# State-space tables of both layers in one feed-forward, and a third feed-forward in seven-product form

## The reference, cut to what matters

```python
x = post_add(x, swiglu(pre(x, 0), ffn_w_in[l, 0], ffn_w_out[l, 0]), 0, 0.5)   # first feed-forward
y = token_mixer(pre(x, 1), ...)       # state-space branch + forgetting attention + gates
x = post_add(x, y, 1, 1.0)
x = post_add(x, swiglu(pre(x, 2), ffn_w_in[l, 1], ffn_w_out[l, 1]), 2, 0.5)   # second feed-forward

def swiglu(h, w_in, w_out):           # 1024 -> 2 x 2816 -> 1024
    gate, up = split(h @ w_in)
    return (silu(gate) * up) @ w_out

def s5_ssm(u, a_re, a_im, log_dt, b_re, b_im, c_re, c_im, d_skip):
    lam = complex(min(a_re, -1e-4), a_im); dt = exp(log_dt)
    lam_bar = exp(lam * dt)
    b_bar = (lam_bar - 1) / lam * b
    states = associative_scan(a2 * a1, a2 * s1 + s2)   # over 512 tokens
    return real(c @ states) + d_skip * u
```

## Time and profile before

| | us |
|---|---|
| median of 3 executions (3386.50 to 3389.12) | 3387.81 |
| profiled execution, its own time | 3392.64 |
| profiled execution, its span | 3390.8 |
| layer 1's first feed-forward: first XH matmul to the next stage's first | 1085.5 to 1468.4 |
| layer 1's second feed-forward | 1875.2 to 2241.3 |
| layer 2's first feed-forward | 2241.3 to 2623.9 |
| layer 2's second feed-forward, from its first XH matmul | about 3029 on |

### The profile page before, as it was taken

One profiled execution on the slowest core, in us unless ns is written; L12 is line 12 of the kernel. 1 busy time (PEld: TensorE's weight loads), 2 busy tenths in 40 slices (PEclk: granted clock), 3 DMA queues, 4 the chain that ended last, 5 costly groups with the idle time before them and its releaser, 6 DMA issues.

```text
span 3390.8 us, 43065 instructions
## 1 busy us (share of the span) xinstructions
PE 3330.1 (98%) x17581; PEld 2689.4 (79%) x17589; DVE 1938.0 (57%) x2745; ACT 1364.9 (40%) x2134; POOL 443.2 (13%) x343
## 2 busy tenths in 40 slices
PE   9999999999999999999999999999999999999998
PEld 6755477688888888888678899978888875879998
DVE  5555666565555635564334867665356633367775
ACT  3374456332223332224533554432323245245443
POOL 0100012222221100122012100020102210220001
PEclk9999999999999999999999999999999999999999
DMA  5412543255553334223033123333432331222232
GB/s 195 148 44 76 186 180 131 105 193 199 194 189 116 122 139 139 87 93 121 31 110 108 57 100 106 101 109 112 146 116 68 123 106 44 100 75 99 95 107 75
DMA packets 82261, 393.68 MB, mean 116 GB/s; under 512 B 8976, under 2 KB 19856, under 8 KB 51088
## 3 DMA queue, kind: packets, MB, share of 16 engines
q1 hardware_dynamic: 69936, 370.41, 30.8%
q10 hardware_dynamic: 12128, 20.52, 1.7%
HBM read 372.02 MB, written 18.87 MB: 115 GB/s over the span
## 4 chain that ended last, share of the span: by engine, by line
PE 90%; DVE 5%; ACT 2%; issue 2%; POOL 0%; DMA 0%; SPq 0%; ACTq 0%; DVEq 0%; POOLq 0%
PE pb L813 16%; PE pb L815 16%; PE pb L814 16%; PE pb L1308 4%; PE pb L1307 4%; PE pb L1306 4%; PE pb L714 2%; PE pb L781 2%; PE pb L716 2%; PE pb L1347 2%; PE pb L1348 2%; PE pb L782 2%; PE pb L1349 2%; PE pb L789 2%; PE pb L1015 1%
## 5 line engine op out<-in xcount | busy, mean ns | idle before, releaser
L2406 DVE TENSOR_TENSOR wl<-w,wh 128x2048 fp32r<-128x2048 f32 (+2 forms) x207 | 449.0, 2169 | 591.3 <-ACT wh L1568 590.7
L813 PE MATMUL pb<-XH,wh 128*128 128x512 f32 (+1 forms) x1848 | 735.4, 398 | 2.3 <-DVE wl L2406 1.6
L815 PE MATMUL pb<-XH,wl 128*128 128x512 f32 (+1 forms) x1848 | 721.3, 390 | 0.0
L814 PE MATMUL pb<-XL,wh 128*128 128x512 f32 (+1 forms) x1848 | 720.7, 390 | 0.0
L1568 ACT ACTIVATE wh<-w 128x2048 fp32r<-128x2048 f32 (+2 forms) x207 | 363.0, 1754 | 217.8 <-PE pb L815 134.5
L813 PEld LDWEIGHTS pb<-XH,wh 128*128 128x128 f32 (+1 forms) x1848 | 345.9, 187 | 83.2 <-issue 8.2
L814 PEld LDWEIGHTS pb<-XL,wh 128*128 128x128 f32 (+1 forms) x1848 | 345.9, 187 | 76.7 <-issue 4.6
L815 PEld LDWEIGHTS pb<-XH,wl 128*128 128x128 f32 (+1 forms) x1848 | 345.3, 187 | 75.6
L2393 DVE CUSTOM_DVE_ANT_0 mreg<-mreg,pr 128x1024 f32<-128x1024 f32 x144 | 196.4, 1381 | 50.4 <-DMA mreg<-in_mod_w 50.1
L813 PE MATMUL pb<-HH,wh 128*128 128x512 f32 x552 | 219.0, 397 | 0.5 <-DVE YT L3356 0.5
L814 PE MATMUL pb<-HL,wh 128*128 128x512 f32 x552 | 218.0, 395 | 0.0
(11 more groups left out here) (589 smaller groups left out, 6507.0 us busy)
## 6 DMA issues: line engine op xcount, KB each, us to landing
mreg<-in_mod_w SPq DMA_DIRECT2D x144, 512.0 KB, 4.1
w<-in_f_in SPq DMA_DIRECT2D x44, 1024.0 KB, 4.8
w<-in_f_wide SPq DMA_DIRECT2D x38, 1024.0 KB, 4.8
w<-in_w_up SPq DMA_DIRECT2D x16, 1024.0 KB, 6.0
w<-in_w_dn SPq DMA_DIRECT2D x16, 1024.0 KB, 5.9
w<-in_f_out SPq DMA_DIRECT2D x16, 1024.0 KB, 4.9
w<-in_m_g SPq DMA_DIRECT2D x16, 1024.0 KB, 4.8
w<-in_f_piece SPq DMA_DIRECT2D x32, 512.0 KB, 3.4
```

The costliest lines, as they stand in the source:

```text
L813: mm(dst, hi[:, cs], xh[:, k, :], start=k == 0, stop=False)
L814: mm(dst, hi[:, cs], xl[:, k, :], start=False, stop=False)
L815: x = mm(dst, lo[:, cs], xh[:, k, :], start=False, stop=fin)
L2406: tt(low[:, 0:s.cols], wslots[b % 3][:, 0:s.cols], h[:, 0:s.cols].bitcast(F32), ALU.subtract).then_inc(*DV.up(("lo", b), ("w_free", b)))
```

## The change

Three things are changed together.

1. `builds()` replaces `ssm_build(l)`: in layer 1's first feed-forward (i = 0) the tables of layer 2 are built first and those of layer 1 behind them. Each engine resumes its generator twice after each tile instead of once. `padded` fills each build up to 66 resumptions.
2. Layer 2's cosine and sine tables are stored to device memory (`ssm_turns`, 2 MB) at resumption 59, and loaded back at the first tile of the last output group of layer 2's first feed-forward. The second build starts behind the store.
3. Layer 2's first feed-forward (i = 2) is added to `WIDE_FFN`. Its first weight block is still split into the extra slot, so the activation sums 2 and 3 are split only when that block is used up.

```diff
-WIDE_FFN = (1, 3)
+WIDE_FFN = (1, 2, 3)
 ...
+BUILD_STORE, BUILD_END = 59, 66
+
+def padded(steps, first, last):
+    n = first
+    for _ in steps:
+        n += 1
+        yield
+    assert n <= last
+    while n < last:
+        n += 1
+        yield
 ...
-                return (pair_high, pair_low) if s.name[1] in WIDE_FFN else (wh_extra, wl_extra)
+                return (pair_high, pair_low) if s.name[1] % 2 else (wh_extra, wl_extra)
 ...
 # PE (and the same on DVE)
+            def builds():
+                yield from padded(ssm_build(1), 0, BUILD_END)
+                yield from padded(ssm_build(0), 0, BUILD_END)
 ...
-                extra = ssm_build(l) if f == 0 else iter(())
+                extra = builds() if i == 0 else iter(())
 ...
                 def after():
                     next(extra, None)
+                    next(extra, None)
 ...
 # ACT
             def wide_first(i):
 ...
                 t_high(1)
-                t_high(3)
+                if i % 2:
+                    t_high(3)
                 unit_high(i, first, "A11", "A12")
-                t_high(2)
+                if i % 2:
+                    t_high(2)
 ...
                 for n in range(2):
                     silu(n, ...)
+                if i % 2 == 0:
+                    act.wait_ge(*at("extra_free", s.name))
+                    t_high(2)
+                    t_high(3)
 ...
             def ssm_build(l):
-                act.wait_ge(*at("extra_free", ("in", 2 * l, 0)))
+                act.wait_ge(*at("extra_free", ("in", 0, 0)))
+                if l == 0:
+                    act.wait_ge(tables_stored, 16)
 ...
+            def builds():
+                yield from padded(ssm_build(1), 0, BUILD_STORE)
+                act.wait_ge(*at("ssm_tables", 1))
+                act.dma_start(ssm_turns, BIG[:, 12288:16384]).then_inc(tables_stored, 16)
+                yield from padded((), BUILD_STORE, BUILD_END)
+                yield from padded(ssm_build(0), 0, BUILD_END)
 ...
                     def y_out(j, o, bank):
 ...
+                        if i == 2 and j == 0:
+                            act.wait_ge(*at("wide_done", 2))
+                            act.dma_start(BIG[:, 12288:16384], ssm_turns).then_inc(tables_landed, 16)
+                        next(extra, None)
                         next(extra, None)
 ...
 # DVE, link into layer 2's first feed-forward
-                if nxt[1] == 2:
+                if nxt[1] == 2 or nxt == (1, 0):
                     t_sums(...)
 ...
 # DVE, mixer of layer 2
+                        if l == 1 and ft == 0:
+                            dve.wait_ge(tables_landed, 16)
```

More of the change, by code:

```diff
@@ L1257, in after @@
                     next(extra, None)
+                    next(extra, None)
                 def after_both():
-                    next(extra, None)
+                    after()
                     sums()
-                if f == 1:
+                if i in WIDE_FFN:
                     run(st_of[("in", i, 0)], XH, XL, xw(r))
@@ L1269, in ffn @@
                     pe.wait_ge(*at("y_piece", i, 15, 1))
-                for q in range(2 * f, 3):
-                    if f == 0:
+                for q in range(2 if i in WIDE_FFN else 0, 3):
+                    if i not in WIDE_FFN:
                         run(st_of[("in", i, q)], XH, XL, xw(r) if q == 0 else None, after)
@@ L1976, in wide_high, with wide_first @@
                     *AC.up(("hh", i, j), *([("hh", i, 2, j - 16)] if j >= 16 else [])))
-            def wide_first(l):
-                i, r = 2 * l + 1, (l, 2)
+            def wide_first(i):
+                r, before = (i // 2, 2 * (i % 2)), (i // 2, 1) if i % 2 else (i // 2 - 1, 2)
                 s = st_of[("in", i, 0)]
@@ L2153, in ffn @@
                 i = 2 * l + f
-                extra = ssm_build(l) if f == 0 else iter(())
-                if f == 1:
-                    wide_first(l)
+                extra = builds() if i == 0 else iter(())
+                if i in WIDE_FFN:
+                    wide_first(i)
                     for j in WIDE_J:
@@ L2171, in in_out @@
                         next(extra, None)
-                    if 0 < q and f == 0:
+                        next(extra, None)
+                    if 0 < q and i not in WIDE_FFN:
                         act.wait_ge(*last_mm(("out", i, q - 1)))
-                    if f == 0:
+                    if i not in WIDE_FFN:
                         run(st_of[("in", i, q)], in_out)
@@ L3116, in slot @@
                     n += 1
-                dve.wait_ge(*at("extra_free", ("in", 2 * l, 0)))
+                r8 = r8s[l]
+                dve.wait_ge(*at("extra_free", ("in", 0, 0)))
+                if l == 0:
+                    dve.wait_ge(tables_stored, 16)
                 v.memset(mt1[:, 0:512], 0.0).then_inc(*DV.up(("zeros", l)))
@@ L3223, in ssm_build @@
                 X, Z = g32(craw[:, 0:512]), g32(craw[:, 512:1024])
[L3224 to L3225 removed]
+                dve.wait_ge(ssm_landed, 16 * (3 * (1 - l) + 2))
+                dve.wait_ge(zero_stored, 16 * 7 * (2 - l))
                 a = g32(mt1[:, 0:512])
@@ L3633, in ffn @@
                 i = 2 * l + f
-                for q, nk in enumerate((8, 8, 6) if f == 0 else ()):
+                for q, nk in enumerate((8, 8, 6) if i not in WIDE_FFN else ()):
                     for j in range(nk):
```

60 lines of the change are left out of this document (30 added, 30 removed).

## The result

The changed kernel takes 3429.1 us (median of 4, 3427.0 to 3429.9), the one before 3387.6 on the same chip: ratio 1.0119, 95% interval 1.0107 to 1.0131, so 41.4 us slower. The forecast was 3415 (range 3386 to 3432), slower.

The account below looks back on a forecast made before the run. PE was taken to bound the kernel (90% of the chain): -12.9 us (8.8 of batches less 21.7 saved) + 28.9 of waits + 10.8 of clock = +26.8 on the median 3387.8, say 3415 us, range 3386 to 3432.

Parts of the forecast that it names:

- the saving: Layer 2's first feed-forward: the seven-product form takes 343.3 us against 365.0 for the plain one, 21.7 less.
- four batches: Host stage (layer 1's first feed-forward): four more turn batches of products and transposes on PE, +8.8 us.
- the waits: Host stage: PE waits caused by the order of the builds at two steps per tile, 28.9 us in sum.
- The places: Waits by host-stage tile (T0 to T67): T10 2.5, T12 0, T13 1.75, T20 0.6, T42 5.5, T43 and T46 1.95 us each.
- The first batch: Layer 2's tables, behind T9: PE waits 11.1 us for DVE's operand, about 4.5 of it before T6.
- the end of the stage: Last three table steps move to T60 and T61 in the host stage: bounds 0 and 9.3 us, 3.5 taken.
- Two of the signs: Expected if right: largest PE wait ahead of the first batch; host stage longer by 35 to 50 us than 365.
- the clock: Half-speed PE behind pauses ahead of six host-stage batches, priced from a link's row at 1.8 us each: 10.8 us.
- The upper bound: Clock loss of 5.4 us per half-speed spell, from the link with a 1.64 us pause; 32 us for six batches.
- DVE keeps up: Faster rival: host-stage stalls before the batches stay under 12.9 us; 3375 us if waits were nil; chance 0.14.
- The slow rival: DVE bounds the whole host stage and the clock falls at each pause, near 0.9: 3444 us; chance 0.16.
- The rival of lower-bound waits: Host-stage waits at their lower bounds, 18 us, clock kept: 3393 us, within 0.2% of before; chance 0.20.

Follow-up runs that it names:

- the best kernel: Kernel of experiment 6 with lag and zero stores issued in two halves and layer 1's first products one resumption later: 3376.9 us.
- the seventh experiment: Two single edits to the changed kernel: zero stores moved behind sine and tanh, 3429.5 us; layer 1's build begun one tile sooner, 3429.5 us.
- experiment 6: Changed kernel with batches respaced, resumption pace evened out, lags' mask in its own place, zero stores later, layer 1's build overlapping layer 2's table store: 3382.7 us.

## Why the prediction was right and where it was off

**Right: the saving.** 21.7 read from the other stage, 21.5 measured; the link at 17.5, the copies of the second and third activation sums hidden, nothing waiting for store or reload (2 MB each, 7.8 us to landing; the prediction had about 9).

**Right: four batches, 8.8 us**, as the best kernel shows (10.0 in all).

**Right: the waits, 28.9 us forecast and 28.9 measured**, partly by luck. The places and the releasers were as worked out (T10 2.5 and 2.6, T13 1.75 and 1.8, T42 5.5 and 5.5, T43 and T46 1.95 and 2.04, T12 0 and 0.2). The first batch was forecast at 11.1 and took 0.96 + 3.29 + 4.62 = 8.9; the end of the stage was forecast at 3.5 and took 5.8. These two errors cancel, with 0.6 at T20 that did not occur. Two of the signs were off for it: the largest single wait was the one ahead of T64 and not ahead of the first batch, and the host stage grew by 61 us and not by 35 to 50. One sentence of the first was wrong too, that DVE works without a pause from the tanh on: it idles for ACT's copies and for PE's tiles, as the seventh experiment shows.

**Off: the clock, 10.8 us in the sum, 23.4 measured.** The term was 6 x 1.8. This is the step that failed. The cause was right, and both factors were too small. Eight places were followed by half speed, not six: T6 and T64 were left out, though I had put waits there myself (3.6 us by my own price). And one spell cost 23.4 / 8 = 2.9 us and not 1.8 (9.0 us over eight); on the kernel before with early batches, 3.3. The row held where no batch stood: the slow matmuls behind the pauses at T6 and T64 lost 1.7 and 2.1 us. My reason for taking it for the batches, that a batch is denser than a link's sums, was no reason for a small price: a batch itself ran at half speed (3.0 to 4.3 for 2.2 us, 1.7 lost on average), and 4 to 11 matmuls behind it as well (0.9 to 2.2 lost). The link's row holds only the matmuls behind. With 23.4 the sum is -12.9 + 28.9 + 23.4 = 39.4, against the 41.4 measured; between the two traces it is 36.5, since the link behind layer 1's second feed-forward came out 3.2 shorter. The upper bound, 5.4 a spell, rested on the link that the trace of after shows at 19.6 instead of 22.8 us; its excess was not steady either. Beside it stood what the Trainium skill says in "TensorE: Matmul & The Clock Gate", Part 1, that the gate puts an idle TensorE at half rate. The traces agree: PE was at half rate behind each pause of 1.82 to 5.84 us in this kernel. So every such pause was to be counted, eight and not six. My reading that every pause would cost went too far: behind 0.17 and 0.96 us nothing was slow. The link's rows were also poor evidence for it, since PE was busy with one- and two-column sums there and not idle (16.48 of 17.6 us).

**The rivals.** "DVE keeps up" turned out true of DVE's capacity and false of this order: at the given pace PE waited 28.9 us, at another the same DVE work let it wait 0.4, and the time came to 3376.9, against 3375 worked out for it. The slow rival (3444, clock near 0.9) was nearer in cause than the forecast, with a cost at every pause; its 5.4 a spell was too high, its first wait and last table steps too, and the clock was 0.94. The rival of lower-bound waits (18 us) fell with the 28.9 measured.

## What to carry to other kernels

When work is interleaved by hand, ask of each hand-over how many tiles lie between the producer's last step and the consumer's first, not how busy the engines are: two resumptions per tile halved that distance. Count each wait on TensorE with the spell behind it, which here cost 0.8 to 1.4 times the wait (28.9 us idle cost 52.3, 19.3 cost 45.8); if a wait can't be removed, throw-away matmuls in it paid in both kernels tried. Moving one late item alone moved the wait, twice; spreading the whole queue removed it.

## What the runs showed of the hardware

- In the changed kernel and in the kernel with early batches a pause of 1.8 to 5.8 us on PE was followed by half speed (1.2 instead of 2.4 GHz): pairs of a batch 0.53 us apart instead of 0.29, then 4 to 11 matmuls of 512 columns at 0.43 us. Behind the 2.04 us at T43 the first five pairs still ran at 0.28 to 0.39; behind the 4.62 at T9 all eight were slow. Behind 0.17 us at T12 and 0.96 ahead of T5 nothing changed, nor behind 1.25 and 1.22 in the kernel of experiment 6. One pause of 1.64, in a link, was followed by a longer slow stretch in one trace than in the other (link 22.8 and 19.6 us).
- Fillers of bf16 matmuls kept the granted clock of the stages at 0.99 (0.94 without them in the changed kernel), and saved 18.3 and 21.7 us in two kernels.
- Eight small stores issued in a row held ACT's queue for up to 9.4 us (experiment 6, first kernel), 6.7 in the kernel before, 5.0 at the least, in the changed kernel; seven took 3.7 to 5.8. A store of 1 or 2 MB held it for 0.33.
